# Splitting the memory as it is loaded and multiplying its norm's root into the key and value products, in a two-block float32 transformer kernel

## The chip, the cores and the metric

The kernel runs on one core of one Trainium2 chip. The metric is the device time of one execution in microseconds (us); the time before is the median of three runs. The profile is one execution recorded by the hardware profiler. Five engines work beside one another: TensorE (PE in the rows, PEld its weight loads), VectorE (DVE), ScalarE (ACT), GpSimd (POOL) and SyncE (SP, which here only issues DMAs). Each runs its own instructions strictly in order and waits on semaphores for the others.

## The reference, cut to what matters

A first block of two attention layers on 1024 tokens of width 1024, then a second block with a pooling mixer and a gated feed-forward. What the change touches is the attention to a memory of 256 tokens, whose keys and values both layers take from one normed memory:

```python
def rmsnorm(x, g):
    xf = x.astype(jnp.float32)
    y = xf * lax.rsqrt(jnp.mean(xf * xf, axis=-1, keepdims=True) + EPS)
    return (y * g.astype(jnp.float32)).astype(x.dtype)

memn = rmsnorm(mem, mem_norm_gain)                    # mem: 256 x 1024
for l in range(2):
    h = rmsnorm(x, norm_gain[l])
    mk, mv = jnp.split(memn @ w_mem_kv[l], 2, axis=-1)  # 512 keys, 512 values
    ...
    ym = memory_attn(qm, mk, mv)
```

The root of the norm is one number per memory token, the gain one number per channel.

## The kernel before, in words

**Products.** A float32 operand is split into a high part (rounded to the type that TensorE multiplies at full rate) and a low part, source minus high part, and a product is three matmuls: high by high, high by low, low by high (`three`, L1935 to L1937). Weights come from HBM in units of 256 KB and are split in halves of 128x256: ACT makes the high part, and DVE and POOL in turn the low part of every other half (`split` steps, L2176 for ACT, L2455 DVE, L2835 POOL). Six places in WS hold split halves, seven raw places (three of WR, two in PY, F1, and SG) hold units as they land. A raw place is loaded again once its unit is split, and a WS place is written again once the matmuls have used it.

**The order of the work.** One Python list `steps` is written by hand-placed calls, and each engine's program walks this list and takes the steps that concern it. So an engine's order is the order of `put` calls. `ahead` puts loads and splits a few halves ahead of the matmuls. `pump` advances the list of dense products by one piece. `first_norm` is a generator of the steps of the norm of x (squares, sums, root, scaling, splitting); the loop near L1885 takes one step of it and then pumps one or two pieces of the memory's products.

**The stage in question.** It is the first stage of the program. DMAs load the memory transposed (MX, two loads of 512 KB), constants, six units of memory weights, x (eight loads of 512 KB), then further weight units as raw places come free. ACT squares the memory's eight chunks of 128 channels and DVE adds the squares up; PE sums over channels (L2105), DVE scales the sums (L2620), POOL takes the power -1/2 (L2824), and PE spreads the root over all partitions into a bank of PSUM (L2119). DVE then forms chunk times gain times root (`nscale`, L2649), ACT takes the high part (`nsplit`, QKV<-EO) and DVE the low part (L2655). Only then do the memory's products begin: per layer four key products (24 matmuls of 256 columns each) and two value products (48 matmuls each), 384 matmuls in all. I call them key products 0 to 3, values 0 and 1 (first layer), key products 4 to 7, values 2 and 3 (second layer). The weights of key product 3 are the seventh unit, which lands in SG behind x. When a product leaves its bank, ACT writes the high part (QKV<-PS) and DVE the low part (L2424).

Between these products stand the steps of the norm of x, in two halves of 512 tokens: squares on ACT (PY<-X), their accumulation on DVE (L2613), sums and root as above (tile SS), scaling and splitting into HT by DVE and ACT. The products of the first attention layer take their moving operand from HT and begin when the memory's products are done.

## Time and profile before

| what | value |
|---|---|
| median of 3 runs | 2355.59 us (2355.25 to 2358.07) |
| profiled execution | 2354.93 us, its span 2353.1 us |
| PE busy | 2271.7 us, 97% |
| DVE busy | 1598.8 us, 68% |
| ACT busy | 1310.6 us, 56% |
| POOL busy | 683.0 us, 29% |
| DMA | 241.68 MB, mean 103 GB/s |

The time of an execution is the span of the engines' work and what lies around it, here 1.8 us. Busy shares are means over the program; the stage that the change touches is the first 75 us, some 3% of the span, and its engines are read from the timeline by themselves.

### The profile page before, as it was taken

The numbers are of one execution on the slowest core, as the hardware profiler recorded it, in microseconds if no ns is written. First come the engines' busy times: TensorE is split into PE (matmuls) and PEld (weight loads), VectorE is DVE, ScalarE is ACT, GpSimd is POOL, SyncE is SP. The second block draws the span as 40 slices with busy tenths as digits, with TensorE's granted clock in tenths as the row PEclk, the third lists the DMA queues.
The fourth block names the chain that finished last, engine by engine and source line by source line (L and its number), as shares of the span: only waits on it lengthen the run. The fifth ranks groups of instructions, "written<-read, shape, count | busy, mean of one in ns | idle before, by whom it ended". The sixth has DMA issues, their size and how long they took to land. (4 is left out here: it accounts for less than half of the span.)

```text
span 2353.1 us, 35362 instructions
## 1 busy us (share of the span) xinstructions
PE 2271.7 (97%) x11778; PEld 1934.2 (82%) x11778; DVE 1598.8 (68%) x3281; ACT 1310.6 (56%) x3022; POOL 683.0 (29%) x843
## 2 busy tenths in 40 slices
PE   7999999999999999999999999898999999999999
PEld 6888888888888878888888888787777888887887
DVE  7444677677885343346666566669788778889787
ACT  6454566666775444456665556655556645455542
POOL 3454332311145642222222222555563200000000
PEclk9999999999999999999999999999999999999999
DMA  7322101111243342222223233523343633345734
GB/s 228 118 72 68 40 25 32 35 36 49 65 137 98 96 130 72 86 75 90 83 91 95 71 94 95 190 86 110 93 139 111 196 96 94 117 143 170 232 113 139
DMA packets 332355, 241.68 MB, mean 103 GB/s; under 512 B 66448, under 2 KB 284816, under 8 KB 331664
## 3 DMA queue, kind: packets, MB, share of 16 engines
q1 hardware_dynamic: 332176, 239.43, 33.6%
q8 instruction: 96, 1.57, 0.3%
q14 instruction: 83, 0.68, 0.1%
HBM read 195.59 MB, written 43.78 MB: 102 GB/s over the span
## 5 line engine op out<-in xcount | busy, mean ns | idle before, releaser
L2835 POOL TENSOR_TENSOR WS<-WR,WS 128x256 fp32r<-128x256 f32 x635 | 493.2, 797 | 1005.3 <-ACT WS L2176 1004.4
L1935 PE MATMUL PS<-HT,WS 128*128 128x512 f32 x1492 | 602.7, 404 | 20.2 <-POOL WS L2835 5.8
L1937 PE MATMUL PS<-HT,WS 128*128 128x512 f32 x1492 | 585.1, 392 | 0.0
L1936 PE MATMUL PS<-HT,WS 128*128 128x512 f32 x1492 | 582.9, 391 | 0.0
L1935 PEld LDWEIGHTS PS<-HT,WS 128*128 128x128 f32 x1492 | 281.4, 189 | 78.2 <-issue 13.4
L1937 PEld LDWEIGHTS PS<-HT,WS 128*128 128x128 f32 x1492 | 280.8, 188 | 61.1
L1936 PEld LDWEIGHTS PS<-HT,WS 128*128 128x128 f32 x1492 | 281.9, 189 | 51.8
L2176 ACT ACTIVATE PT<-PS 128x512 fp32r<-128x512 f32 x352 | 185.9, 528 | 198.9 <-PE PS L2048 198.4
L2176 ACT ACTIVATE WS<-WR 128x256 fp32r<-128x256 f32 x658 | 245.3, 410 | 81.9 <-PE PS L1937 55.2
L2424 DVE TENSOR_TENSOR PT<-PS,PT 128x512 fp32r<-128x512 f32 x352 | 211.1, 609 | 84.7 <-ACT PT L2176 81.8
L2081 PE MATMUL PS<-PT,QKV 128*128 128x256 f32 (+1 forms) x1248 | 208.4, 289 | 3.2 <-DVE YB L2603 2.4
L2176 ACT ACTIVATE QKV<-PS 64x512 fp32r<-64x512 f32 (+2 forms) x208 | 121.6, 585 | 140.4 <-PE PS L1937 119.1
L2081 PEld LDWEIGHTS PS<-PT,QKV 128*128 128x128 f32 x1248 | 178.0, 191 | 9.2 <-ACT PT L2176 3.8
L2048 PE MATMUL PS<-ID,PY 128*128 128x128 f32 x1072 | 182.9, 274 | 0.1
L2425 DVE SCALAR_TENSOR_TENSOR QKV<-PS,QKV 64x512 fp32r<-64x512 f32 (+1 forms) x112 | 77.1, 689 | 109.9 <-ACT QKV L2176 107.7
L2176 ACT ACTIVATE PY<-PY,ST 128x384 f32<-128x384 f32 (+1 forms) x192 | 115.7, 602 | 37.6 <-DVE ST L2554 25.5
L2534 DVE TENSOR_REDUCE ST<-PS 128x1 f32<-128x256 f32 (+1 forms) x128 | 102.2, 819 | 45.8 <-PE PS L2036 24.0
L2547 DVE CUSTOM_DVE_ANT_0 PY<-PS,EO 128x384 f32<-128x384 f32 (+1 forms) x192 | 103.5, 539 | 42.0 <-PE PS L2036 41.4
L2035 PE MATMUL PS<-QKV 128*128 128x384 f32 (+2 forms) x320 | 120.7, 378 | 8.4 <-ACT PY L2176 7.0
L2048 PEld LDWEIGHTS PS<-ID,PY 128*128 128x128 f32 x1072 | 127.6, 141 | 0.6 <-ACT PY L2176 0.4
L2424 DVE TENSOR_TENSOR QKV<-PS,QKV 64x512 fp32r<-64x512 f32 (+2 forms) x96 | 63.9, 666 | 92.3 <-ACT QKV L2176 91.1
L2176 ACT ACTIVATE X<-PS 128x512 f32<-128x512 f32 (+1 forms) x128 | 66.0, 543 | 98.1 <-PE PS L2167 57.9
(282 smaller groups left out, 4585.4 us busy)
## 6 DMA issues: line engine op xcount, KB each, us to landing
WR<-in_w_in_odd SPq DMA_DIRECT2D x106, 256.0 KB, 2.9
EO<-in_grid SPq DMA_DIRECT2D x48, 384.0 KB, 3.1
WR<-in_ffn_in SPq DMA_DIRECT2D x60, 256.0 KB, 3.0
WR<-in_w_in_even SPq DMA_DIRECT2D x100, 128.0 KB, 2.5
WR<-in_w_out_odd SPq DMA_DIRECT2D x48, 256.0 KB, 2.9
yd<-PY SPq DMA_DIRECT2D x44, 256.0 KB, 3.3
EO<-in_ffn_in SPq DMA_DIRECT2D x35, 256.0 KB, 3.1
WR<-in_w_in_even SPq DMA_DIRECT2D x34, 256.0 KB, 2.9
```

What stands on the lines that cost most here:

```text
L1935: e.matmul(out, wh, rh, start=start, stop=False)
L1936: e.matmul(out, wh, rl, start=False, stop=False)
L1937: return e.matmul(out, wl, rh, start=False, stop=stop)
L2035: e.matmul(out, q, kh, start=True, stop=False)
L2048: m = e.transpose(PS[:, B_PT + pb, o + 128 * z:o + 128 * z + 128], p_at(job.c, job.scores[x].slot, p0, p0 + 128), ID[:, :])
L2081: m = e.matmul(out, vv, p, start=a, stop=b)
L2176: return e.activation(out, in_, func, **more)
L2424: return e.tensor_tensor(out, src, f32(hi), ALU.subtract)
L2425: return e.scalar_tensor_tensor(out=out, in0=src, scalar=scale, in1=f32(hi), op0=ALU.mult, op1=ALU.subtract)
L2534: e.tensor_reduce(st[:, 1:2], src, AX.XY, ALU.max, negate=True).then_inc(s_mx.sem, 1)
L2547: e.tensor_tensor_reduce(out=two_parts(p, s.cut), in0=src, in1=two_parts(bias, s.cut), scale=1.0, scalar=NEG, op0=ALU.add, op1=ALU.max, ac ...
L2835: e.tensor_tensor(ws(i, 1, n), RAW[raw_slot(u)][:, o:o + n], f32(ws(i, 0, n)), ALU.subtract).then_inc(s_wlop.sem, 1)
```

## The change: what it does

1. The memory is split as it lands, times its gain and without the root (`mem split`): ACT writes the high part of each chunk from MX with the gain as its scale, DVE the low part in one instruction. The eight `nscale` steps of the memory are gone.
2. The memory's squares, sums and root come later, between key products. `rootless` holds the products that are already computed but may not leave their bank before the root is known. A new step `mem root` copies the root, spread over partitions, from PSUM to MROOT.
3. When a key product leaves its bank, DVE first multiplies it with MROOT into MK (in EO), then ACT takes the high part from MK, then DVE the low part. For a value product the root is one number per partition: ACT and DVE take it as their scale, in two instructions each, one per tile of 128 tokens.
4. The order of the first loads: first half of the memory, the columns of gains, first weight unit, second half of the memory, the other constants, five units, x. PE and ACT wait for the constants later than before.
5. The loop near L1885 pumps a second piece only from its 17th step on.

```diff
-        MRING = [EO[:, 2048 + 256 * i:2304 + 256 * i] for i in range(4)]
+        MROOT = EO[:, 2048:2304]
+        MK = [EO[:, 2304 + 256 * i:2560 + 256 * i] for i in range(2)]
...
+                if rootless is not None:
+                    rootless.append(h)
+                    return
...
-        for c in range(8):
-            square(mem_norm, c, (d_mem[c // 4], 16))
-        for _ in range(6):
+        load_next()
+        put("constants")
+        for _ in range(5):
             load_next()
         put("x load")
+        for c in range(4):
+            mem_split(c)
+        ahead(3 - NSPL)
+        for c in range(4, 8):
+            mem_split(c)
+        for c in range(0, 8, 2):
+            pump()
+            square(mem_norm, c, (d_mem[c // 4], 16))
+            square(mem_norm, c + 1, (d_mem[c // 4], 16))
+        flush_acc()
+        pump()
         closing = close(mem_norm)
         next(closing)
-        ahead(0)
+        next(closing)
+        pump()
         for _ in closing:
             pass
-        for _ in norm_split(mem_norm, C_MEMG, mem_at, MRING, [], [(d_mem[1], 16)] * 8):
-            pass
+        put("mem root")
+        halves_done, rootless = rootless, None
+        for h in halves_done:
+            leave(h)
+        pump()
+        pump()
...
         for i, _ in enumerate(first_norm()):
-            for _ in range(1 + i % 2):
+            for _ in range(1 + i % 2 * (i > 15)):
...
# ACT, a weight split
-                    w.wait_ge(d_const, 64)
+                    w.wait_ge(d_col, 16)
+                    w.wait_ge(d_const, 48)
# ACT, a value product and a key product leave
-                        act(hi, src).then_inc(s_ea.sem, 1)
+                        w.wait_ge(s_pow, mem_norm.rstd)
+                        for t in (0, 1):
+                            act(hi[:, :, t], src[:, :, t], scale=SM[:, 4 + t:5 + t]).then_inc(s_ea.sem, 1)
...
-                        act(k_at(slot, 0, 0, m0, m0 + 256), ps, scale=1.0).then_inc(s_ea.sem, 1)
+                        w.wait_ge(s_ed, h.ed + 1)
+                        act(k_at(slot, 0, 0, m0, m0 + 256), MK[h.to[4] % 2], scale=1.0).then_inc(s_ea.sem, 1)
# ACT, new steps
+                    act(mem_at(0, c), MX[:, c, :], scale=COL[:, C_MEMG + c:C_MEMG + c + 1]).then_inc(s_nh.sem, 1)
+                    act(MROOT, PS[:, B_O, 0:MEM]).then_inc(s_mroot.sem, 1)
# DVE, a key product leaves
-                        w.wait_ge(s_ea, h.ea + 1)
-                        take(k_at(slot, 0, 1, m0, m0 + 256), ps, k_at(slot, 0, 0, m0, m0 + 256)).then_inc(s_ed.sem, 1)
+                        m0, t = 256 * h.to[4], MK[h.to[4] % 2]
+                        w.wait_ge(s_mm, h.no)
+                        w.wait_ge(s_mroot, 1)
+                        e.tensor_tensor(t, ps, MROOT, ALU.mult).then_inc(s_ed.sem, 1)
+                        w.wait_ge(s_ea, h.ea + 1)
+                        take(k_at(slot, 0, 1, m0, m0 + 256), t, k_at(slot, 0, 0, m0, m0 + 256)).then_inc(s_ed.sem, 1)
# SP
+            mem_load(0)
+            e.dma_start(COL[:, :], d["cols"]).then_inc(d_col.sem, 16)
             for kind, *of in steps:
+                if kind == "constants":
+                    mem_load(1)
+                    e.dma_start(ID[:, :], d["ident"]).then_inc(d_const.sem, 16)
```

**ACT's queue around the seventh weight unit.** Before, from the last splits of the first weight units to the unit in SG (QKV<-EO are the memory's chunks, PY<-X the squares of x, WS the weight splits, QKV<-PS the key products that leave):

```order
L2176 ACTIVATE WS<-PY 128x256 [waits s_wused,d_raw3]
L2176 ACTIVATE PY<-X 128x512 [waits s_sums,d_x0]
L2176 ACTIVATE WS<-PY 128x256 [waits s_wused]
L2176 ACTIVATE QKV<-PS 128x256 [waits s_mm]
L2176 ACTIVATE PY<-X 128x512 [waits s_acc,d_x1]
L2176 ACTIVATE WS<-PY 128x256 [waits s_wused,d_raw4]
L2176 ACTIVATE WS<-PY 128x256
L2176 ACTIVATE PY<-X 128x512 [waits s_acc,d_x2]
L2176 ACTIVATE WS<-F 128x256 [waits s_wused,d_raw5]
L2176 ACTIVATE PY<-X 128x512 [waits s_acc,d_x3]
L2176 ACTIVATE WS<-F 128x256 [waits s_wused]
L2176 ACTIVATE QKV<-PS 128x256 [waits s_mm]
```

The next row there is the first split from SG. In the changed kernel the same stretch reads, up to the first two squares of x:

```order
L2212 ACTIVATE EO<-PS 128x256 [waits s_bcast]
L2212 ACTIVATE QKV<-EO 128x256 [waits s_ed]
L2212 ACTIVATE WS<-F 128x256 [waits s_wused,d_raw5]
L2212 ACTIVATE WS<-F 128x256 [waits s_wused]
L2212 ACTIVATE QKV<-EO 128x256 [waits s_ed,s_mm]
L2212 ACTIVATE WS<-SG 128x256 [waits s_wused,d_raw6]
L2212 ACTIVATE WS<-SG 128x256
L2212 ACTIVATE PY<-X 128x512 [waits s_sums,d_x0]
L2212 ACTIVATE WS<-WR 128x256 [waits s_wused,d_raw0]
L2212 ACTIVATE PY<-X 128x512 [waits s_acc,d_x1]
```

All squares of x now stand behind the splits of the unit in SG (d_raw6 is its landing); four stood ahead of them. L2212 is the changed file's line for L2176.

**DVE's queue where a key product of the second layer leaves.** Before (key product 4):

```order
L2455 TENSOR_TENSOR WS<-F,WS 128x256 [waits d_raw5,s_whi]
L2424 TENSOR_TENSOR QKV<-PS,QKV 128x256 [waits s_ea]
L2649 SCALAR_TENSOR_TENSOR EO<-X,COL,PS 128x512 [waits d_x3]
L2655 TENSOR_TENSOR HT<-EO,HT 128x512 [waits s_nh]
L2613 TENSOR_TENSOR PY<-PY 128x512 [waits s_acc,s_sq]
```

and in the changed kernel:

```order
L2505 TENSOR_TENSOR WS<-F,WS 128x256 [waits d_raw5,s_whi]
L2532 TENSOR_TENSOR EO<-PS,EO 128x256 [waits s_mm]
L2474 TENSOR_TENSOR QKV<-EO,QKV 128x256 [waits s_ea]
L2711 SCALAR_TENSOR_TENSOR EO<-X,COL,PS 128x512 [waits d_x3]
L2717 TENSOR_TENSOR HT<-EO,HT 128x512 [waits s_nh]
```

The multiplication stands directly ahead of the low part, and the wait between them (s_ea) is for ACT's high part, which is itself made from the multiplication's output. The neighbours are the same. On PE only three small steps move: the memory's sums and root go from ahead of all products to among key product 1, and the sums of the first half of x stand six matmuls later.

## Rows read from the trace of the kernel before

**Rows 1.** The page's first part: busy time, share of the span, instructions.

```profile
PE 2271.7 (97%) x11778; PEld 1934.2 (82%) x11778; DVE 1598.8 (68%) x3281; ACT 1310.6 (56%) x3022; POOL 683.0 (29%) x843
```

**Rows 2.** Stretches: bounds, length, busy PE, PEld, DVE, ACT, POOL, clock, DMA, GB/s.

```profile
34.10:44.40 10.30, 10.26 (x86) 10.08 (x86) 7.61 (x14) 6.29 (x16) 5.16 (x6) 1.00 0.60 174
44.40:60.70 16.30, 12.91 (x98) 11.77 (x96) 16.30 (x30) 11.55 (x31) 5.72 (x7) 1.00 0.36 110
60.70:76.70 16.00, 13.96 (x102) 12.82 (x103) 14.71 (x27) 10.59 (x26) 8.59 (x11) 1.00 0.24 72
```

**Rows 3.** Timeline of PE: start, duration, operation, idle time before it and its releaser.

```profile
13.66 0.55 PE L1935 MATMUL PS<-QKV,WS 128*128 128x256 f32 x1 [1.78 <-DVE QKV L2655]
...
14.23 0.42 PE L1937 MATMUL PS<-QKV,WS 128*128 128x256 f32 x1
14.45 0.43 PE L1935 MATMUL PS<-QKV,WS 128*128 128x256 f32 x1
...
20.09 0.28 PE L1935 MATMUL PS<-QKV,WS 128*128 128x256 f32 x1
20.21 0.28 PE L1936 MATMUL PS<-QKV,WS 128*128 128x256 f32 x1
...
25.55 0.36 PE L1935 MATMUL PS<-QKV,WS 128*128 128x256 f32 x1 [0.26 <-issue]
...
62.01 0.65 PE L2119 MATMUL PS<-ID,SS 128*128 128x128 f32 x4 [1.37 <-POOL SS L2824]
...
74.65 0.40 PE L1935 MATMUL PS<-HT,WS 128*128 128x512 f32 x1
```

**Rows 4.** DMA issues on the timeline, landing of SG's loads, and ACT's wait for it.

```profile
8.09 4.16 SPq L2894 DMA_DIRECT2D X<-in_xT  x8
12.29 0.43 SPq L2906 DMA_DIRECT2D SG<-in_w_mem  x1
...
DMA to landing us min/median/max: 2.6/3.0/11.5
...
SK<-in_sink SPq DMA_DIRECT2D x1, 4.0 KB, 3.9
...
23.80 0.42 ACT L2176 ACTIVATE WS<-SG 128x256 fp32r<-128x256 f32 x1 [0.83 <-DMA SG<-in_w_mem]
```

**Rows 5.** Timeline of ACT: first and fourth square of x, a later weight split.

```profile
17.79 0.62 ACT L2176 ACTIVATE PY<-X 128x512 f32<-128x512 f32 x1
...
21.77 0.62 ACT L2176 ACTIVATE PY<-X 128x512 f32<-128x512 f32 x1
...
29.59 0.71 ACT L2176 ACTIVATE WS<-PY 128x256 fp32r<-128x256 f32 x2
```

**Rows 6.** Timeline of DVE: sums of squares, value product 0 leaves, second half's statistics.

```profile
21.76 1.83 DVE L2613 TENSOR_TENSOR PY<-PY 128x512 f32<-128x512 f32 x2
...
24.18 0.68 DVE L2613 TENSOR_TENSOR PY<-PY 128x512 f32<-128x512 f32 x1
...
37.09 0.69 DVE L2424 TENSOR_TENSOR QKV<-PS,QKV 128x512 fp32r<-128x512 f32 x1 [1.20 <-ACT QKV L2176]
...
60.60 0.15 DVE L2620 TENSOR_SCALAR SS<-PS 128x4 f32<-128x4 f32 x1
```

**Rows 7.** Timeline of DVE and ACT: one chunk scaled, then its high part.

```profile
16.34 0.48 DVE L2649 SCALAR_TENSOR_TENSOR EO<-EO,COL,PS 128x256 f32<-128x256 f32 x1
...
16.85 0.42 ACT L2176 ACTIVATE QKV<-EO 128x256 fp32r<-128x256 f32 x1 [0.31 <-DVE EO L2649]
```

**Rows 8.** Timeline of ACT and DVE: key product 4 leaves its bank.

```profile
46.53 0.36 ACT L2176 ACTIVATE QKV<-PS 128x256 fp32r<-128x256 f32 x1
...
48.07 0.41 DVE L2424 TENSOR_TENSOR QKV<-PS,QKV 128x256 fp32r<-128x256 f32 x1
```

**Rows 9.** Timeline of PE after a long wait in a later stage.

```profile
164.72 0.47 PE L1935 MATMUL PS<-HT,WS 128*128 128x512 f32 x1 [2.36 <-DVE SG L2472]
165.03 0.40 PE L1936 MATMUL PS<-HT,WS 128*128 128x512 f32 x1
165.26 0.40 PE L1937 MATMUL PS<-HT,WS 128*128 128x512 f32 x1
```

More of the change, by code:

```diff
@@ L485, in leave @@
                 a, v = a // 2, v // 2
+            if h.rhs[0] == "mem":
+                v = 2
             if h.kind in ("v", "rope"):
@@ L509, in leave @@
             h.end = (s_ea if h.kind in ("v", "vg", "rope") else s_ed, (s_ea if h.kind in ("v", "vg", "rope") else s_ed).n)
+            if h.rhs[0] == "mem":
+                h.end = (s_ed, h.ed + 1)
             if h.kind in ("k", "kg"):
@@ L1288, in first_half @@
                 yield
-                yield from norm_split(x_norm[0], C_G0, ht_half(0), HRING, [(s_nd, 8)], xt)
+                yield from norm_split(x_norm[0], C_G0, ht_half(0), HRING, [(s_nlv, 8), (s_sums, 1)], xt)
             split = first_half()
@@ L2120, in tensor_program @@
                     m.then_inc(s_bcast.sem, 1)
+                    if nm is mem_norm:
+                        until[nm.bank] = (s_mroot, 1)
+                        continue
                     until[nm.bank] = (s_nd, nm.nd[7]) if not both else (s_pd, blocks[nm.bank - B_S, 7].scaled)
@@ L2322, in scalar_program @@
                         act(YS[:, i, 0:nm.n], nm.src(c), ACT.Square, scale=scale).then_inc(s_sq.sem, 1)
+                elif kind == "mem split":
+                    c, = of
+                    w.wait_ge(d_mem[c // 4], 16)
+                    w.wait_ge(d_col, 16)
+                    act(mem_at(0, c), MX[:, c, :], scale=COL[:, C_MEMG + c:C_MEMG + c + 1]).then_inc(s_nh.sem, 1)
+                elif kind == "mem root":
+                    w.wait_ge(s_bcast, mem_norm.bcast)
+                    act(MROOT, PS[:, B_O, 0:MEM]).then_inc(s_mroot.sem, 1)
                 elif kind == "nsplit":
@@ L2422, in take @@
             def take(out, src, hi, scale=1.0):
-                if scale == 1.0:
+                if isinstance(scale, float) and scale == 1.0:
                     return e.tensor_tensor(out, src, f32(hi), ALU.subtract)
@@ L2474, in vector_program @@
                         src, hi, lo = mem_v_parts(h)
[L2475 to L2480 removed]
+                        w.wait_ge(s_ea, h.ea + 2)
+                        for t in (0, 1):
+                            take(lo[:, :, t], src[:, :, t], hi[:, :, t], SM[:, 4 + t:5 + t]).then_inc(s_ed.sem, 1)
+                    elif h.kind == "hl" and h.rhs[0] == "mem":
+                        m0, t = 256 * h.to[4], MK[h.to[4] % 2]
+                        w.wait_ge(s_mm, h.no)
+                        w.wait_ge(s_mroot, 1)
+                        e.tensor_tensor(t, ps, MROOT, ALU.mult).then_inc(s_ed.sem, 1)
+                        w.wait_ge(s_ea, h.ea + 1)
+                        take(k_at(slot, 0, 1, m0, m0 + 256), t, k_at(slot, 0, 0, m0, m0 + 256)).then_inc(s_ed.sem, 1)
                     elif h.kind == "hl":
@@ L2636, in vector_program @@
                     e.tensor_tensor(nm.stat[:, 12:16], nm.stat[:, 12:16], nm.stat[:, 4:8], ALU.mult).then_inc(s_var.sem, 1)
+                elif kind == "mem split":
+                    c, = of
+                    w.wait_ge(d_mem[c // 4], 16)
+                    w.wait_ge(d_col, 16)
+                    w.wait_ge(s_nh, mem_norm.nh[c])
+                    take(mem_at(1, c), MX[:, c, :], mem_at(0, c), COL[:, C_MEMG + c:C_MEMG + c + 1]).then_inc(s_nlv.sem, 1)
                 elif kind == "nscale":
```

26 lines of the change are left out of this document (14 added, 12 removed).

## The prediction

> **What bounds the kernel now.** I read the page's busy times first: PE works 97% of the span [rows 1], so a stage gains only by PE's idle time in it, and what comes after the first 75 us is untouched: its instructions and their order are the same. What counts is when PE can begin the products on HT, now at 74.65 [rows 3]. A microsecond there is a microsecond of the kernel.
>
> Second, PE's timeline of the first stage. Its first product waits until 13.66 for the first chunk of the normed memory [rows 3]. That is the idle time at which the change aims. After that, 384 matmuls of 256 columns are spaced 0.22 us at first (14.23 to 14.45) and 0.12 us later (20.09 to 20.21) [rows 3]; the granted clock reads 1.00 in every stretch, while the spacing is that of 1.2 GHz and then of 2.4 GHz. At 0.12 us they need 46 us, but PE takes 61 from 13.66 to 74.65. So something else holds it, and the table of stretches shows what: from 44.4 to 60.7 DVE is busy 16.30 of 16.30 us, and in the next 16 us 14.71 [rows 2]. DVE carries the norm of x, the low parts of half the weights and the low parts of all that leaves. PE waits 1.37 us at 62.01 for the root of x's second half [rows 3], whose statistics DVE reaches at 60.60 [rows 6]. From 34.1 to 44.4 DVE has 2.7 us to spare (7.61 busy of 10.30) [rows 2].
>
> Third, the loads. The seventh weight unit (SG) is issued at 12.29 behind x, lands 11.5 us later, and ACT waits for it until 23.80 [rows 4]. Key product 3 needs it and starts at 25.55 [rows 3]. The load, not PE, already sets that start.
>
> **The change, part by part.**
>
> *An earlier first product.* The first matmul no longer waits for squares, sums, root and scaling. It waits for one split chunk and one split weight half. The first weight split still waits for all constants; the last of them lands 3.9 us after its issue [rows 4], at about 7, and one weight load of 256 KB is now ahead of it. Bounds: 7 and 13.66; I take 9, a gain of about 4.7 us at this point. Nothing else rests on the value, because of the next item.
>
> *The gain ends at the seventh unit.* Key products 0 to 2 took 11.9 us from 13.66 to 25.55 [rows 3]. The memory's sums and root now fall among them and may cost 2.5 us of waiting. From 9 on, PE is through at about 23. But SP issues the same twenty loads ahead of SG as before, without a wait, so SG lands at about 23.8 again and key product 3 starts near 25.5 again. PE then idles some 2.4 us. Term: 0. Bounds: a gain of 0.3 to a loss of 0.3. The eight scalings that the memory loses on DVE fall into this stretch too and are worth nothing for the same reason.
>
> *PE's clock in that gap.* After a wait of 2.36 us in a later stage the next matmul followed after 0.31 us and the one behind it after 0.23 us [rows 9], so the clock had not fallen. The term is 0. The Trainium skill, "TensorE: Matmul & The Clock Gate", Part 1 (the two states), says that an idle array falls back to half rate; by that rule key product 3 would run at the early spacing of 0.22 us [rows 3], 24 matmuls or 2.4 us later, of which the wait for the next weight halves would hide most.
>
> *The squares of x move behind the wait.* Before, four of x's eight first squares ran on ACT from 17.79 to 22.4 [rows 5], and DVE had added three of them up before 25 (1.83 and 0.68, together 2.5 us) [rows 6]. Now all eight stand behind the splits of SG, so none runs before 24.4. From there ACT has eight squares and eight weight splits, and a square with a split took 0.83 us (0.52 and 0.31, start to start): 6.6 us. Two leaving key products in between hold it for about 0.9 us each. The pair of weight splits that ran at 29.59 [rows 5] moves to about 32.4, its low part is ready at about 33.5, and PE, which used that half at 32.5, loses about 1.1 us; value product 0 then leaves at 38.3 to 38.5 instead of 37.09 [rows 6]. Bounds: 0, if DVE's 2.7 us of slack up to 44.4 [rows 2] takes up the 2.5 us; and 4.3, if nothing does and both held products (2 times 0.9) come on top. I take 1.3, because up to 44 PE and ACT pace one another and DVE's slack takes up only its own share.
>
> *The multiplication with the root.* The rows of before show no such operation. The nearest is the chain of scaling and high part of one memory chunk: ACT starts 0.51 us after a DVE instruction of 0.48 us and takes 0.42 [rows 7]. A multiplication from PSUM is like the low part at 48.07, 0.41 us [rows 8], so the low part may start 0.44 + 0.42 = about 0.87 us later than if ACT had been done. And ACT had been done: it wrote the high part at 46.53, 1.5 us ahead of DVE's low part at 48.07 [rows 8]. That lead is lost, since the high part now needs DVE's product, and DVE, with the low part next in its queue, stands still meanwhile. Per key product DVE loses 0.87 us (bounds: 0.33, if only the slot of the added instruction counted, and 1.2, if ACT comes 0.3 late). Key products 4, 5 and 6 leave between 44.4 and 60.60, where DVE has nothing to spare: 3 times 0.87 = 2.6 us (bounds 1.0 and 3.6). Products 0 to 3 are in the items above. Product 7 leaves while DVE waits for the second root, and costs nothing. If that cover went, 0.87 more.
>
> *Values.* A value product leaves in two instructions of 256 instead of one of 512, 2 times 0.41 against 0.69 [rows 6, 8], on ACT likewise. Value 2 leaves while DVE is almost full: 0.3 us (bounds 0.1 and 0.6). Values 0 and 1 are in the 1.3; value 3 is the last work of the stage and HT's halves are done by then.
>
> *The last item of the diff* keeps the position of x's norm among PE's products nearly as it was; the order of the instructions shows this, so it has no term of its own. SP's stores of keys and values, and the loads behind them, shift with value 3.
>
> **Sum.** 0 + 1.3 + 2.6 + 0.3 = 4.2 us later at the first matmul on HT, 78.8 to 78.9 in place of 74.65. The profiled execution took 2354.93 us, so 2359.1 us. The median of the runs is 0.7 us above that execution, which I leave in the range. A measurement of this kernel tells a difference from none from about 0.2% on, 4.7 us.
>
> **The rivals.**
>
> *The lead is kept (faster).* If SG landed 4 us earlier, or x's norm could use the early start, the whole stage would follow the first matmul. For it: PE stands idle for 13.66 us and the stage is nowhere bound by the weight loads after SG. Against it: SG's 11.5 us to landing and ACT's wait at 23.80 [rows 4], and DVE's full stretches [rows 2], in which the change adds work. It gives 2354.9 - 4.7 = 2350.2 us. Chance 14%.
>
> *The slack hides it (no change).* The squares come late, but DVE's 2.7 us take them up, and each multiplication costs its slot only: 0 + 1.0 + 0.1, about 2356 us. For it: the idle time in the stretch up to 44.4. Against it: DVE's low part is directly behind the multiplication. Chance 15%.
>
> *The held copy makes the weights late (slower).* ACT reached key product 4's copy 1.5 us early and used the lead for weight splits. Now it stands at the copy until DVE comes, and all splits behind it are later by the lead and by 0.87 us. Where PE has less than about 2 us of split halves in hand, it waits for them, sends its release of WS places later, and the splits slip again. With 0.9 us more at each of the three products this is 4.2 + 2.7 = 6.9, 2361.8 us. For it: at 62.01 and before PE is already the one that waits. Against it: the wait at 62.01 (1.37 us) [rows 3] gives PE a little room there. It decides against me from half a microsecond on. Chance 33%.
>
> **How the numbers follow.** My forecast has 38%. It and the hidden case lie within 0.2% of 2355.59: 53%. Slower by over 0.2%: 33%; faster by over 0.2%: 14%. The range must reach into both outer cases; 2351.5 to 2362.0 leaves out most of the faster case and the worst of the slower one, about 2 in 10. The bounds of my own terms, all at one end together, are +0.8 and +8.8 us (2355.7 and 2363.7); the range takes in all of it but the last 1.7 us, since the high ends exclude one another in part. The likeliest case by itself spans 2357.5 to 2360.3.
>
> **What would show it.** In the profile of the changed kernel: first matmul at 8.5 to 9.5; ACT waiting for SG until about 23.8 and key product 3 starting near 25.4 after an idle PE; x's first square after 24.4; ACT's QKV<-EO copies waiting for DVE, and DVE's low part waiting for ACT, 0.4 to 0.5 us each; statistics of the second half at about 64.5 in place of 60.60, and the first matmul on HT at about 78.9. I am wrong if SG lands well before 23, if the statistics of the second half come before 61, or if DVE shows idle time between 45 and 60 other than at the copies.

## The result and the profile after

| | median | runs |
|---|---|---|
| kernel before | 2356.83 us (2355.25 to 2358.48) | 4 |
| changed kernel | 2370.01 us (2365.78 to 2371.11) | 4 |

The ratio is 1.0051, 95% interval 1.0039 to 1.0063: by the medians the change costs 13.2 us. I had forecast 2359.1 and a range up to 2362.0. A later comparison, with the two kernels run in turn, gave 2368.91 against 2357.30, ratio 1.0051 (1.0035 to 1.0067), 11.6 us.

The profiled execution took 2371.11 us, 16.2 more than that of before. The page's first part, which answers to [rows 1]:

```profile
PE 2283.1 (96%) x11778; PEld 1942.8 (82%) x11778; DVE 1602.4 (68%) x3285; ACT 1312.8 (55%) x3027; POOL 683.9 (29%) x843
```

DVE has 3.6 us more work, yet the kernel lost 13. So the added work alone is not the loss; what it does to waiting has to be read. PE's timeline, the first matmul, then the last three ahead of key product 3 and its first:

```profile
10.80 0.55 PE L1968 MATMUL PS<-QKV,WS 128*128 128x256 f32 x1 [10.80 <-POOL WS L2897]
...
27.26 0.28 PE L1968 MATMUL PS<-QKV,WS 128*128 128x256 f32 x1
27.38 0.28 PE L1969 MATMUL PS<-QKV,WS 128*128 128x256 f32 x1
27.50 0.28 PE L1970 MATMUL PS<-QKV,WS 128*128 128x256 f32 x1
27.62 0.28 PE L1968 MATMUL PS<-QKV,WS 128*128 128x256 f32 x1
```

PE starts 2.9 us earlier than before, and 17 us later it is 2.1 us behind (27.62 against 25.55 [rows 3]), without having waited in front of that product. (This holds for this execution; in a second profile of the same kernel, experiment 5, key product 3 starts at 25.58, as before.) The first matmul on HT starts at 84.85 in place of 74.65: 10.2 us. The three stretches of [rows 2], and two of 8 us in which the clock fell:

```profile
34.10:44.40 10.30, 8.28 (x69) 7.92 (x68) 8.30 (x15) 8.83 (x24) 5.96 (x7) 1.00 0.44 127
44.40:60.70 16.30, 12.23 (x93) 11.19 (x93) 14.60 (x25) 8.47 (x22) 4.59 (x6) 1.00 0.40 114
60.70:76.70 16.00, 13.95 (x90) 13.57 (x90) 14.21 (x25) 9.74 (x25) 7.35 (x9) 0.79 0.21 67
18.00:26.00 8.00, 7.15 (x35) 7.15 (x36) 3.63 (x8) 2.41 (x8) 2.27 (x4) 0.57 1.07 371
62.00:70.00 8.00, 7.35 (x36) 7.38 (x37) 7.35 (x16) 4.09 (x11) 2.93 (x4) 0.57 0.24 72
```

From 44.4 to 60.7 DVE is 1.7 us short of full and ACT does 3.1 us less than before: both stand, and PE stands with them. In the last two stretches the granted clock is 0.57: it is 0.50, the level of 1.2 GHz, from 18.7 to 25.5 and from 63.1 to 69.9. In the kernel before it fell nowhere in the stage once the matmuls had reached the fast spacing (at 19.5 us).

Where the two stand shows in the timelines of DVE, ACT and GpSimd, as key product 5 leaves (DVE multiplies, ACT copies, DVE takes the low part):

```profile
60.00 0.42 DVE L2532 TENSOR_TENSOR EO<-PS,EO 128x256 f32<-128x256 f32 x1
60.96 0.43 DVE L2474 TENSOR_TENSOR QKV<-EO,QKV 128x256 fp32r<-128x256 f32 x1 [0.55 <-ACT QKV L2212]
...
60.51 0.42 ACT L2212 ACTIVATE QKV<-EO 128x256 fp32r<-128x256 f32 x1 [3.50 <-DVE EO L2532]
...
61.83 0.73 POOL L2897 TENSOR_TENSOR WS<-WR,WS 128x256 fp32r<-128x256 f32 x1 [4.83 <-ACT WS L2212]
```

DVE waits 0.55 us for ACT. ACT has waited 3.50 us for DVE, and GpSimd 4.83 us for ACT's next weight split.

In the rest of the program the loss grows from 10.2 to 16.2 us. It grows in steps of 1.0 to 1.7 us, at stretches in which the clock falls (below).

### The profile page after: what moved, and what is told of

Read it like the earlier page. It is cut to its first block and busy times, and to the rows that moved or that the text cites. A ratio compares the mean times of both kernels' runs of the same rounds, so it can differ in the third digit from the quotient of the medians.

```text
span 2369.3 us, 35384 instructions
## 1 busy us (share of the span) xinstructions
PE 2283.1 (96%) x11778; PEld 1942.8 (82%) x11778; DVE 1602.4 (68%) x3285; ACT 1312.8 (55%) x3027; POOL 683.9 (29%) x843
## 5 line engine op out<-in xcount | busy, mean ns | idle before, releaser
L1968 PE MATMUL PS<-HT,WS 128*128 128x512 f32 x1492 | 603.0, 404 | 20.5 <-POOL WS L2897 5.7
L2212 ACT ACTIVATE PT<-PS 128x512 fp32r<-128x512 f32 x352 | 186.2, 529 | 201.0 <-PE PS L2080 200.6
L2212 ACT ACTIVATE WS<-WR 128x256 fp32r<-128x256 f32 x658 | 245.6, 410 | 86.3 <-PE PS L1970 58.3
L2212 ACT ACTIVATE QKV<-PS 64x512 fp32r<-64x512 f32 (+1 forms) x196 | 116.4, 594 | 137.5 <-PE PS L1970 116.0
L2212 ACT ACTIVATE PY<-PY,ST 128x384 f32<-128x384 f32 (+1 forms) x192 | 115.6, 602 | 37.5 <-DVE ST L2608 25.5
L2212 ACT ACTIVATE X<-PS 128x512 f32<-128x512 f32 (+1 forms) x128 | 66.0, 542 | 97.3 <-PE PS L2203 55.3
L2474 DVE TENSOR_TENSOR QKV<-PS,QKV 64x512 fp32r<-64x512 f32 (+1 forms) x84 | 57.9, 689 | 91.2 <-ACT QKV L2212 90.0
```

Of the source, the lines that this page charges most:

```text
L1968: e.matmul(out, wh, rh, start=start, stop=False)
L2212: return e.activation(out, in_, func, **more)
L2474: return e.tensor_tensor(out, src, f32(hi), ALU.subtract)
```

## The experiments

Every median is given against the kernel before in the same comparison (2357.0 to 2358.7 us), with the ratio and its 95% interval. The ratio is not the quotient of the two medians; in 13 the two differ most (10.6 us by the medians, 13 by the ratio). "HT" is the start of the first matmul on HT in the profile of one execution, 74.65 before and 84.85 and, in the second profile, 83.79 in the changed kernel. It is one execution's number and carries what the clock did in it: the median is the measure of a version, HT says where the time goes.

**1. The key products without the multiplication** (changed kernel).

```diff
-                        w.wait_ge(s_ed, h.ed + 1)
-                        act(k_at(slot, 0, 0, m0, m0 + 256), MK[h.to[4] % 2], scale=1.0).then_inc(s_ea.sem, 1)
+                        act(k_at(slot, 0, 0, m0, m0 + 256), ps, scale=1.0).then_inc(s_ea.sem, 1)
...
-                        e.tensor_tensor(t, ps, MROOT, ALU.mult).then_inc(s_ed.sem, 1)
```

> The changed kernel, but the key products leave their banks as in the kernel before, without the multiplication with the root (the root is left out of the keys, so this is the price of the hand-off alone). My theory, the sum of hand-offs, displaced squares and a late memory root: the first matmul on HT comes 4 to 5 us earlier than in the changed kernel (84.85), at about 80 to 81; ACT's idle time ahead of the key copies is gone; the time falls by 4 to 7 us, to 2363 to 2366. Rival, TensorE's half clock in the stage alone makes the delay: HT moves by less than 1.5 us. Rival, the weights come late because ACT stands at the held copy: 6 us or more come back, HT at 79 or earlier.

Measured: 3.7 us over before (1.0018, 1.0009 to 1.0027), HT at 80.27. The multiplication is worth 8 of the 12 to 13 us, more than the 4 to 7 that I had expected; about 4 remain. HT came as my theory had it, and TensorE was at half clock for as long ahead of HT here as in the second profile of the changed kernel (10.2 us, table below), so the rival of the clock fails.

**2. The kernel before with a multiplication by ones in the same place.**

```diff
+                        e.tensor_tensor(t, ps, YB[:, :], ALU.mult).then_inc(s_ed.sem, 1)
...
-                        act(k_at(slot, 0, 0, m0, m0 + 256), ps, scale=1.0).then_inc(s_ea.sem, 1)
+                        w.wait_ge(s_ed, h.ed + 1)
+                        act(k_at(slot, 0, 0, m0, m0 + 256), MRING[h.to[4] % 2], scale=1.0).then_inc(s_ea.sem, 1)
```

> The kernel before, with one thing added: when a key product leaves, DVE first multiplies it with a tile of ones into EO, and ACT takes the high part from there. Order of loads, squares and norm are as before. My theory: the hand-offs of products 4 to 7 make the first matmul on HT 3.5 to 4.5 us later than 74.65, at 78.2 to 79.2, and the time 2358.5 to 2361. Rival, the hand-off costs only its slot on DVE (0.41 us each): HT at 76 to 76.5. Rival, the delay in the changed kernel is mostly the order of loads and the early start: HT moves by less than 1 us. Rival, the loss behind the stage comes from later clock falls that any shift of the stage sets off: the time rises by 5 us more than HT does.

Measured: 6.4 us over before (1.0026, 1.0016 to 1.0036), HT at 83.30 in the profile, which was its slowest execution (2368.24; the median is 2364.18). The hand-off alone, with order, loads and squares as before, makes half of the loss. Both numbers lie past what I had expected (HT up to 79.2, time up to 2361), since I had counted products 4 to 7 alone. The timelines of DVE and ACT:

```profile
51.94 0.41 DVE L2484 TENSOR_TENSOR EO<-PS,YB 128x256 f32<-128x256 f32 x1
52.90 0.43 DVE L2427 TENSOR_TENSOR QKV<-EO,QKV 128x256 fp32r<-128x256 f32 x1 [0.54 <-ACT QKV L2178]
58.65 0.41 DVE L2484 TENSOR_TENSOR EO<-PS,YB 128x256 f32<-128x256 f32 x1
59.60 0.43 DVE L2427 TENSOR_TENSOR QKV<-EO,QKV 128x256 fp32r<-128x256 f32 x1 [0.54 <-ACT QKV L2178]
...
59.15 0.42 ACT L2178 ACTIVATE QKV<-EO 128x256 fp32r<-128x256 f32 x1 [3.50 <-DVE EO L2484]
```

From key product 4 to key product 7 DVE takes 16.70 us here, 16.71 in the changed kernel, and 12.93 before (48.07 to 61.00), with the same other instructions. The changed kernel's two ends of this interval are

```profile
53.29 0.41 DVE L2532 TENSOR_TENSOR EO<-PS,EO 128x256 f32<-128x256 f32 x1
...
70.00 0.41 DVE L2532 TENSOR_TENSOR EO<-PS,EO 128x256 f32<-128x256 f32 x1
```

The 3.78 us of three hand-offs, by DVE's rows of the changed kernel (start to start, by kind): 1.63 of waiting, 1.24 in the slots of the multiplications, and 1.03 in HT's low parts and the squares' sums (7.06 us against 6.03 for the same nine), less 0.1 in the rest. So one costs 1.26 us; I had taken 0.87.

**3. Four squares of x ahead of the root's copy** (changed kernel).

```diff
         for _ in closing:
             pass
+        for c in range(4):
+            square(x_norm[0], c, xt[c])
         put("mem root")
```

> The changed kernel with the first four squares of x put back ahead of the copy of the root, where ACT idles for 4 us (17.8 to 21.8); the rest is as in the change. My theory: value product 0 leaves DVE 2 to 3 us earlier than 41.86, the first matmul on HT at 82 to 83 in place of 84.85, the time 2 to 3 us lower. Rival, the delay is set by the seventh weight unit and DVE's hand-offs: HT moves by less than 0.7 us. Rival, the squares wait for x, which now lands later, and hold up the copy of the root: HT no earlier, key product 3 later than 27.62.

Measured: 10.0 us over before (1.0041, 1.0027 to 1.0055), HT at 82.83, value product 0 leaves at 39.86. Against the two profiles of the changed kernel that is 1.0 to 2.0 us at either point, against its two medians 1.6 to 3.2. The size forecast was 1.3. But the interval overlaps with that of the changed kernel (1.0035 to 1.0067), and this profile had no clock fall ahead of 55 us, while the other two had one near 19 us. So the direction is likely, and the size is not shown by this pair; 6 against 4 below (4.4 against 8.3) says the same again.

**4. The multiplication apart**: a step of its own on DVE that frees the bank; ACT's copy and DVE's low part one piece of the products later.

```diff
+        def mem_key(h):
+            mem_multiply(h)
+            yield False
+            yield False
+            leave(h)
```

> The changed kernel with the multiplication as a step of its own that frees the bank, and the high and low part one piece of the products later, so that ACT and DVE do other work in between and do not stand waiting for one another. Same instructions. My theory: of 0.96 us a hand-off the 0.54 us of waiting goes, for products 4 to 7 and 2 to 3; the first matmul on HT 2 to 3 us earlier than 84.85; ACT's idle time ahead of the copies (8.9 us in four) is below 2 us. The time 2 to 4 us lower. Rival, what costs is the added DVE instruction: HT moves by less than 0.7 us. Rival, weights late from ACT's stand at the copy: HT 4 us or more earlier.

Measured: 8.3 us over before (1.0033, 1.0020 to 1.0046), HT at 82.16. Product 4 to 7 take 13.95 us, so three hand-offs cost 1.0 us in place of 3.8. ACT still stood 4.7 us ahead of the four copies of products 4 to 7 (8.9 in the changed kernel), where I had expected below 2.

**5. The changed kernel again.**

> The changed kernel itself once more, to tell what in its trace repeats. My theory: the intervals set by the order of work repeat within 0.3 us (three hand-offs from key product 4 to 7 in 16.7 us; first matmul on HT 14.5 to 15.3 us after the second half's statistics); what does not repeat is where TensorE's granted clock is 0.50 behind the stage (45 us in the first trace, 32 in the kernel before), and so the part of the loss that came after 85 us (6 of 16 us) shrinks to 0 to 4. The time is 9 to 13 us over the kernel before. Rival, the clock falls are a consequence of the change: again 50 us or more at half clock and 5 us or more lost after the stage.

Measured: 11.6 us over before; HT at 83.79, product 4 to 7 again 16.70 us, HT again 15.26 us behind the second half's statistics (before 14.05, in 1 without the multiplication 14.24, in 2 with it 15.07). The multiplication of product 7 stands in those last 15 us: it costs 1.0 us (against 1, and 2 against before), where I had 0.

These two profiles also show what the clock does to the second half of the stage. From product 4's multiplication to product 7's PE was at half clock for 6.8 us in the first and 3.4 us in the second, and the interval is 16.71 and 16.70; from there to HT it was 0 and 3.4 us, and the interval is 14.85 and 14.86. So behind product 4 the clock does not set the pace. Ahead of it, it does in part: key product 3 starts at

```profile
25.58 0.36 PE L1968 MATMUL PS<-QKV,WS 128*128 128x256 f32 x1
```

in the second profile, where the clock was at 0.50 from 19.1 to 22.5 (3.4 us), and at 27.62 in the first, with 6.8 us; 0.9 of these 2.0 us come from a later first matmul (10.80 against 9.89). The loss of the second profile against before builds up behind that start: 3.7 us where value product 0 leaves (40.81 against 37.09), 4.2 at product 4 (52.23 against 48.07), 7.9 at product 7, 9.1 at HT.

**6 to 8. Apart and squares ahead; the same with the seventh unit ahead of x; and the changed kernel with the old rule of the loop.**

```diff
# 7, besides
-        for _ in range(5):
+        for _ in range(6):
             load_next()
# 8, alone
-            for _ in range(1 + i % 2 * (i > 15)):
+            for _ in range(1 + i % 2):
```

> The multiplication apart and the four squares of x ahead, both in one kernel. In one look each they made the first matmul on HT 2.7 and 2.0 us earlier than 84.85. My theory: the two act at different places, so they add: HT at 79.5 to 80.5, the time 4 to 7 us over the kernel before. Rival, they share one bound (ACT's queue up to 40 us): HT at 81.5 to 82.5 and nothing gained over the multiplication apart alone.

> As the kernel with both, and the seventh weight unit loaded ahead of x instead of behind it. My theory: ACT no longer waits for it (25 us), key product 3 leaves 1 to 2 us earlier, x lands 0.7 us later, which the squares bear; the first matmul on HT 0.5 to 2 us earlier than with both alone. Rival, DVE and ACT are full from there on anyway: no difference in HT. Rival, x lands late and the squares ahead of the root's copy hold it up: HT later.

> The changed kernel with the old rule in the loop that mixes x's norm into the products (a second piece of the products in every other step from the start, not from the 17th on). The norm of x then stands later among the products. My theory: x's norm is what ends the stage, so it comes out later or the same: HT at 84.5 to 88, the time 0 to 3 us over the changed kernel. Rival, PE starves because the norm's steps crowd the weight splits: HT earlier by 1 us or more.

Measured: 4.4 us over before (1.0018, 1.0009 to 1.0026), HT 79.67; 3.9 (1.0016, 1.0008 to 1.0025), HT 79.46; 6.4 (1.0023, 1.0012 to 1.0034), HT 82.00. The first two edits add. The seventh unit adds nothing that shows. The old rule, which I had taken to be harmless or worse, gives 5 us: it is the rival that was nearer. With it the second half's statistics come at 74.52, later than the 68.5 to 69.6 of the changed kernel, and HT still comes earlier. What differs is where DVE finishes x's second half. In the kernel before and in the changed one only two of its instructions start after HT has begun (both are low parts, the last three of which start from 74.30 and 84.50 on). With the old rule in the changed kernel 11 of them do, 7.6 us of DVE's time, and the last ends at 90.9:

```profile
87.75 0.68 DVE L2717 TENSOR_TENSOR HT<-EO,HT 128x512 fp32r<-128x512 f32 x1
88.36 0.74 DVE L2711 SCALAR_TENSOR_TENSOR EO<-X,COL,PS 128x512 f32<-128x512 f32 x1
89.02 1.89 DVE L2717 TENSOR_TENSOR HT<-EO,HT 128x512 fp32r<-128x512 f32 x3
```

They run beside products that need only the first half of HT.

**9 to 12. Everything removed; the seventh unit early in the kernel before and in the changed kernel; all edits with the old rule.** Number 9 is experiment 1 with the squares and the seventh unit ahead, 12 is experiment 7 with the old rule.

> Without the multiplication (the root is left out of the keys, as before), with the squares of x ahead, and the seventh weight unit ahead of x: all that I hold for the cause of the delay is taken out together. My theory: nothing of size is left, the first matmul on HT at 75 to 77 (before: 74.65) and the time within 3 us of the kernel before; the 3 us by which the first matmul comes earlier than before are worth nothing here either. Rival, something unnamed (the late root, the order of the loads) costs besides: HT at 78 or later. Rival, the early start shows now: HT at 73 or earlier.

> The kernel before with one edit: the seventh weight unit is loaded ahead of x. ACT waits 0.83 us for it there and key product 3 starts at 25.55. My theory: key product 3 starts about 1 us earlier, but x lands 0.7 us later and its squares with it, and DVE is full from 44 on; HT 0 to 1 us earlier, the time within 2 us. Rival, all behind follows the load: 2 us or more gained. Rival, x is what matters and is now late: slower by 0.5 to 1 us.

> The changed kernel with the seventh weight unit ahead of x alone. My prediction held that this unit sets key product 3's start. If so, key product 3's multiplication comes 1 to 2 us earlier than 32.5 to 33.5 and HT 1 to 2 us earlier than 84. Rival, in the changed kernel the late root and the two held products set it, and the unit is there anyway when ACT comes: less than 0.7 us at both.

> The kernel with all three edits (multiplication apart, four squares ahead, seventh unit ahead of x) and the old rule of the loop, which by itself made the changed kernel 5 us faster against my expectation. If the old rule acts by keeping DVE's work on x's norm out of the stretch from 44 to 68 us, it adds to the three: HT at 77 to 78.5, the time within 0 to 3 us of the kernel before. Rival, it gains only where the hand-offs stall DVE, and is worth nothing or harms once they are apart: HT at 79.5 or later.

Measured: 9: 3.7 us over before (1.0016, 1.0007 to 1.0025), HT 77.41. 10, the kernel before with the unit early: 0.9 (1.0000, 0.9991 to 1.0009), HT 74.17. 11, the changed kernel with it: 11.4 (1.0051, 1.0038 to 1.0064), HT 87.71, key product 3 multiplied at 33.41 against 33.54 and 32.47. 12: 0.7 (1.0005, 0.9996 to 1.0014), HT 75.20, better than I had expected (77 to 78.5).

In 11 the time is that of the changed kernel; its HT is 3 to 4 us later in an execution that was at half clock for 20.5 us ahead of HT (13.7 and 10.2 in the other two). By product 4 it was already 2.5 us behind the first profile (55.78 against 53.29); I take that for the clock's. In 9, a little past my theory (77 at most, 3 us): without the multiplication nearly 3 us of HT were left, and the early start was worth nothing. Number 12 has all eight multiplications and is level with the kernel before. It differs from 7 in the rule alone, so the remaining piece was the rule. DVE's timeline of 12 behind HT's start at 75.20:

```profile
76.06 0.73 DVE L2728 SCALAR_TENSOR_TENSOR EO<-X,COL,PS 128x512 f32<-128x512 f32 x1
76.72 0.68 DVE L2734 TENSOR_TENSOR HT<-EO,HT 128x512 fp32r<-128x512 f32 x1
...
80.63 0.73 DVE L2728 SCALAR_TENSOR_TENSOR EO<-X,COL,PS 128x512 f32<-128x512 f32 x1
81.29 1.88 DVE L2734 TENSOR_TENSOR HT<-EO,HT 128x512 fp32r<-128x512 f32 x3
```

Ten instructions of x's norm, 6.4 us, start behind the stage there. Number 10 says that SG's landing, which I had taken for the gate of key product 3, is worth 0.5 us in the kernel before (key product 3 starts at 25.08, HT comes at 74.17) and nothing that the time shows.

**13 to 15. Fewer low parts of the weights on DVE in the memory's products**, in the changed kernel, in version 12 and, as the control, in the kernel before.

```diff
-                    on = s_wlov if no % (2 if no < 2 * MEM_UNITS else 3) else s_wlop
+                    on = s_wlov if (no % 3 == 1 if no < 2 * MEM_UNITS else no % 3) else s_wlop
```

> The changed kernel with fewer low parts of the weights on DVE in the memory's products (every third half instead of every second; GpSimd has the rest). The order of everything else is kept. My theory: DVE's work and stalls between 50 and 70 us are what the stage waits for, some 10 low parts at 0.4 us leave DVE, and the first matmul on HT comes 2 to 4 us earlier than 84. Rival, the hand-off holds ACT and through it the weights, DVE's load matters little: HT within 1 us of 84. Rival, GpSimd's low parts at 0.8 us come late and PE waits for them: HT later.

> The kernel with the three edits and the old rule of the loop, which was level with the kernel before (HT at 75.20), and in it the same shift of weight low parts from DVE to GpSimd. If DVE is still the bound there, HT comes 1 to 3 us earlier and the kernel beats both, by 1 to 3 us. Rival, GpSimd's parts come late: HT at 76 or later, slower than the kernel before.

> The kernel before with the same shift of weight low parts from DVE to GpSimd: the control. If DVE's full stretch from 44.4 to 60.7 bounds the kernel before too, as my prediction had it, HT comes 1 to 3 us earlier than 74.65 and the time 1 to 3 us lower. Rival, PE and the weights bound it: no change or 1 to 2 us slower.

Measured, in this order: 10.6 us over before (1.0055, 1.0042 to 1.0068), HT 82.39; 3.7 (1.0020, 1.0009 to 1.0030), HT 78.68; -0.9 (0.9996, 0.9987 to 1.0005), HT 74.06. The shift bought nothing that can be measured in 13 and 15, against what I had expected, and 14 came out rather worse than 12. Product 4 to 7 took 16.23 us in 13, and 13.20 in 15 where the kernel before took 12.93. DVE was without a pause there in 15 too, with two low parts of the weights less; but its HT low parts and the squares' sums took 6.98 us in place of 6.03, because more of them ran beside GpSimd (last section). So the experiment did not take the load away, it turned it into longer instructions. That DVE sets the pace from 44 to 61 is not refuted by it, and 8 and 12 speak for it; it is not shown by an experiment that takes load off DVE, since none of these did.

**16. The new rule of the loop alone, in the kernel before.**

> The kernel before with the changed kernel's rule in the loop (second piece of the products from the 17th step on). My prediction gave this edit no term, and in the changed kernel the old rule was 5 us faster. If pushing x's norm ahead of the products costs by itself: HT at 77 to 80 and the time 2 to 5 us over the kernel before. Rival, it costs only where the hand-offs already crowd DVE: HT within 1 us of 74.65 and the time within 2 us.

Measured, as expected: 2.3 us over before (1.0013, 1.0004 to 1.0022), HT 78.13. The second half's statistics come at 55.91 instead of 60.60, the products later: key product 4 leaves at 54.04 instead of 48.07. DVE is through with x's norm at 73.4 here and HT comes at 78.13. So an earlier norm doesn't bring the stage's end nearer; my reading is that it takes DVE and ACT from the weights that PE needs. In the kernel before the rule costs 2.3 us, in the changed kernel 5.2 (8).

**17. Which of the two stands counts**: DVE's order as in experiment 4, but ACT's copy directly behind the multiplication. **18. Apart and the old rule**, nothing else.

```diff
# 17
             put("mem multiply", h)      # DVE multiplies, ACT copies
             yield False
             yield False
             put("mem low", h)
```

> As the kernel with the multiplication apart, and DVE's order is the same as there; but ACT's copy stands directly behind the multiplication, as in the changed kernel, and only DVE's low part comes later. So DVE doesn't wait for ACT, while ACT still stands at the copy until DVE multiplies. If ACT's stand and the weight splits queued behind it make a hand-off dear: from key product 4's multiplication to product 7's still 16 us or more, HT within 1 us of 84. If DVE's wait does: about 14 us, as apart, and HT at 82.

> The multiplication apart and the old rule of the loop, without the squares ahead and without the early seventh unit: the smallest repair. Alone they gave 3 and 5 us. If they add: HT at 78 to 80, the time 2 to 5 us over the kernel before; the squares ahead and the early unit then account for the last 2 to 3 us of the version that was level. Rival, the two cure the same stall: HT at 81 or later.

Measured, 17: product 4 to 7 in 15.57 us, between 16.70 (joined) and 13.95 (apart); 6.8 us over before (1.0028, 1.0018 to 1.0037), HT 81.23. ACT's copies of products 4 to 6, first of 17, then of 4:

```profile
51.85 0.42 ACT L2221 ACTIVATE QKV<-EO 128x256 fp32r<-128x256 f32 x1 [2.08 <-DVE EO L2700]
57.98 0.42 ACT L2221 ACTIVATE QKV<-EO 128x256 fp32r<-128x256 f32 x1 [2.93 <-DVE EO L2700]
63.69 0.42 ACT L2221 ACTIVATE QKV<-EO 128x256 fp32r<-128x256 f32 x1 [1.65 <-DVE EO L2700]
```

```profile
53.86 0.42 ACT L2223 ACTIVATE QKV<-EO 128x256 fp32r<-128x256 f32 x1 [1.87 <-DVE EO L2704]
59.45 0.42 ACT L2223 ACTIVATE QKV<-EO 128x256 fp32r<-128x256 f32 x1 [0.39 <-DVE EO L2704]
64.57 0.42 ACT L2223 ACTIVATE QKV<-EO 128x256 fp32r<-128x256 f32 x1 [1.35 <-DVE EO L2704]
```

In that stretch DVE's wait accounts for 1.1 us and ACT's stand for 1.6. In the whole time 17 and 4 can't be told apart (6.8 and 8.3 over before, the intervals overlap), since 17 was 2 us ahead when product 4 left. Neither of the two expected outcomes came: both stands cost in this stretch, and their shares in the total stay open. 18: 3.1 us over before (1.0012, 1.0003 to 1.0020), HT 77.96: the two edits add. The squares ahead and the early unit are then what is left to 12, 2.4 us by the medians of two comparisons, whose intervals overlap.

**What came after the stage.** Time at half clock (from a table of stretches of 4 us each, twice the share of the clock that is missing) ahead of HT and behind 92 us, and the time from HT to the end of the span:

| profile | HT | half clock ahead of HT | HT to end | half clock behind 92 |
|---|---|---|---|---|
| before | 74.65 | 0 | 2278.5 | 31.8 |
| changed | 84.85 | 13.7 | 2284.5 | 45.4 |
| changed, again | 83.79 | 10.2 | 2282.6 | 35.0 |
| 1, no multiplication | 80.27 | 10.2 | 2280.0 | 35.0 |
| 2, ones | 83.30 | 10.2 | 2283.1 | 38.4 |
| 3, squares | 82.83 | 6.8 | 2279.7 | 31.9 |
| 4, apart | 82.16 | 6.8 | 2279.1 | 28.7 |
| 6, both | 79.67 | 3.4 | 2279.0 | 31.8 |
| 7, all three | 79.46 | 10.2 | 2279.9 | 28.6 |
| 8, old rule | 82.00 | 10.2 | 2280.1 | 28.4 |
| 9, everything removed | 77.41 | 3.4 | 2283.1 | 33.6 |
| 10, before, unit early | 74.17 | 0 | 2282.1 | 31.9 |
| 11, changed, unit early | 87.71 | 20.5 | 2280.2 | 35.4 |
| 12, all, old rule | 75.20 | 3.4 | 2281.5 | 35.4 |
| 13, changed, shift | 82.39 | 3.4 | 2284.1 | 30.2 |
| 14, 12 with shift | 78.68 | 10.2 | 2283.4 | 35.1 |
| 15, before, shift | 74.06 | 3.4 | 2283.6 | 31.8 |
| 16, before, new rule | 78.13 | 3.4 | 2281.3 | 31.7 |
| 17, low part later | 81.23 | 6.8 | 2281.9 | 28.4 |
| 18, apart, old rule | 77.96 | 3.4 | 2282.2 | 35.1 |

The rest of the program differs by up to 6 us, and follows neither HT nor any edit. In the first profile of the changed kernel the clock can account for it: 13.6 us more at half rate are 6.8 us at most, and the rest is 6.0 us longer. In the second it can't: 3.2 us more at half rate are 1.6 us at most, and the rest is 4.1 us longer. Nor in 10, which runs the kernel before with one load moved: the same time at half clock, and 3.6 us longer. The profile of before is the shortest of all here, and the experiments from 9 on ran on other chips than 1 to 8, so one profile against another says little at this size. The medians say 12 to 13 us where HT says 9.1 to 10.2. The clock alone varies among runs of one kernel too: the changed kernel's four runs had mean clocks of 0.994, 0.991, 0.989 and 0.988 and took 2365.78, 2369.44, 2370.57 and 2371.11 us. So of the 16.2 us between the first two profiles 10.2 belong to the stage; what makes the rest of it is in part the clock and stays open otherwise. Whether the change makes clock falls behind the stage more frequent is open. Inside the stage it seems to: one begins between 18 and 22 us in 12 of the 15 profiles with the changed order of the first loads and of the memory's norm, and in none of the 5 with the order of before.

## Why the prediction was wrong, point by point

- **An earlier first product, worth nothing.** Right. The first matmul came at 10.80 and 9.89 (forecast 9, bounds 7 and 13.66), and with everything else removed (9) HT was still not early. PE had not been idle for all of the 13.66 us before, as I wrote: the memory's sums and root took 1.7 of them.
- **"The gain ends at the seventh unit", term 0.** The start was right, the reason wrong. In the second profile key product 3 starts at 25.58, as forecast, in the first at 27.62, with the first matmul 0.9 us later and 3.4 us more at half clock. In neither did it wait for SG: ACT took SG's first half at 25.33, directly behind the held copy at 25.00 (24.25 and 23.62 in the second), and loading the unit ahead of x changed nothing in the time (11). What ACT had waited for there is the late root: its copy ran at 21.81, after ACT had idled for 4.02 us (20.43 and 3.54). The term is 0.0 to 2.1 us; the loss that repeats builds up behind this start.
- **PE's clock, term 0.** The clock did fall, though not in the gap that I had looked at: it was granted at 0.50 from 18.7 to 25.5, where PE was busy for 6.65 of 6.80 us at the slow spacing, behind a wait of 2.13 us for the sums at 18.85. By the Trainium skill, "TensorE: Matmul & The Clock Gate", Part 1 (the two states), an idle array falls back to half rate. The trace agrees here and at the start of both kernels, where the first matmuls are 0.21 to 0.22 us apart (the 1.00 that the profile prints for that start is not what they ran at); in [rows 9] it doesn't, the array stayed fast behind a wait of 2.36 us. What the fall cost at this place is not separated: key product 3 was multiplied at 33.54 and 32.47 in the two profiles of the changed kernel, and at 31.74 in 13, which had no fall ahead of 68 us but also fewer low parts on DVE.
- **The displaced squares, 1.3.** Right in kind as far as is shown; the size came out as 1.0 to 2.0 in 3, with the clock mixed in.
- **The multiplication, 2.6 for three and 0 for product 7.** This is the first step that failed: the mechanism was right, size and reach were wrong. Start to start it was 0.95 us (0.91 to 0.96 in all eight), near my 0.87, but each of the three cost 1.26 by what it set off, 3.8 together. Product 7 cost 1.0 where I had DVE's waiting for the root as its cover. And the first four, which I had put under other items, cost as much again (in experiment 2 DVE came to product 4 at 51.94 instead of 48.07, 3.9 us late). Together 6.4 us by medians in the kernel before, 8 in the changed kernel, in place of 2.6.
- **The rule of the loop, no term.** The second step that failed. I had read "order kept" as "costs nothing", and the rule costs 2.3 us by itself in the kernel before (16) and 5.2 in the changed kernel (8). There DVE, with eight multiplications and their waits more, finished x's second half 10 us later, and the stage with it. The old rule lets much of that work run out behind the stage, where DVE has room (5.07 us busy of the 25 from 75 on, in the kernel before).
- **"DVE is full from 44.4 to 60.7."** Stands: the account in experiment 2 closes on DVE's own rows, and two different courses of the clock leave it as it is (5). The way out that it suggests, giving its work to GpSimd, failed (13 to 15).
- **The rivals.** "The held copy makes the weights late" (33%, 2361.8) named what happened: ACT stood 1.6 to 3.5 us at each copy of the second layer, and the splits behind it were late (GpSimd waited 4.83 us for one). It priced that at 0.9 us more at three products and stayed 8 us short. "The lead is kept" and "the slack hides it" fell.

By medians the hand-offs are worth 6 to 8 us, the norm's place 2 to 5, the squares some 2 to 4 with wide intervals. These overlap, since the parts are not independent; all edits together bring the kernel from 12 us over to level (12). No version was measurably faster than the kernel before.

## What to carry to other kernels

Before an operation is put between two engines that used to work on the same source side by side, look at how far ahead the second one was and what stands behind it in its queue: the lead is lost with everything that lived on it, here weight splits for the engine that bounds the program. If it must be there, give it a step of its own and let both engines do other work between its parts. And when one engine of a stage gets more to do, ask which of its work the next stage can still take, and place that anew: the same order of instructions is no longer the same schedule.

## What the runs showed of the hardware that I had not expected

TENSOR_TENSOR instructions of DVE that read two operands from SBUF are stretched when a GpSimd instruction runs beside them and began first. In the changed kernel's timelines of DVE and GpSimd:

```profile
52.35 0.68 DVE L2667 TENSOR_TENSOR PY<-PY 128x512 f32<-128x512 f32 x1
...
56.31 1.23 DVE L2667 TENSOR_TENSOR PY<-PY 128x512 f32<-128x512 f32 x1
67.51 0.69 DVE L2717 TENSOR_TENSOR HT<-EO,HT 128x512 fp32r<-128x512 f32 x1
...
56.25 0.74 POOL L2897 TENSOR_TENSOR WS<-WR,WS 128x256 fp32r<-128x256 f32 x1 [0.41 <-ACT WS L2212]
67.52 1.27 POOL L2897 TENSOR_TENSOR WS<-PY,WS 128x256 fp32r<-128x256 f32 x1 [3.50 <-ACT WS L2212]
```

The same addition takes 0.68 us alone and 1.23 beside GpSimd's 0.74. At 67.51 DVE began first: it kept its 0.69 us, and GpSimd's low part took 1.27. In the first 92 us of this profile 34 such DVE instructions overlap with a low part of the weights on GpSimd by more than 0.2 us. In the 9 where DVE began first it kept its length and GpSimd took 0.81 to 1.27 us; of the 25 where GpSimd began first, 24 DVE instructions were longer than alone. The scalings that read PSUM (EO<-X,COL,PS) kept 0.66 us start to start in every kernel. The Trainium skill, "GPSIMD Engine Reference", Key points, says that the two engines share interfaces to SBUF and contend where a VectorE instruction has two inputs there; the trace agrees. It accounts for the part of a hand-off above its own 0.95 us in the rows of experiment 2, and for what took back the gain in 15.
